# Second block's up projections: one 512-column matmul for both parts of the activation, and a reduction that adds the halves

## The reference, cut to what matters

```python
def swiglu(h, w_gate, w_up, w_down):
    return (jax.nn.silu(h @ w_gate) * (h @ w_up)) @ w_down
...
        h = rmsnorm(x, norm_ffn_pre[layer])
        f = swiglu(h, ffn_w_gate[layer], ffn_w_up[layer], ffn_w_down[layer])
        x = x + rmsnorm(f, norm_ffn_post[layer]).astype(x.dtype)
```

## Time and profile before

| | |
|---|---|
| time, median of 3 runs (lowest to highest) | 1777.63 us (1777.48 to 1779.65) |
| the profiled execution: its own time, its span | 1778.24 us, 1776.3 us |
| granted TensorE clock, mean over the span | 0.981 of full |
| TensorE busy (matmul) | 1696.2 us, 95% |
| TensorE weight loads (beside the matmuls) | 1645.0 us, 93% |
| VectorE busy | 1167.0 us, 66% |
| ScalarE busy | 812.7 us, 46% |
| GpSimd busy | 237.9 us, 13% |
| DMA, mean | 157 GB/s |

### The profile page before, as it was taken

The page is one execution under the profiler, slowest core; times in us unless marked ns, Lnnn a source line. Parts: engine busy times, 40 slices in busy tenths (PEclk is TensorE's granted clock), DMA queues, the critical chain, the costliest instruction groups (busy, mean ns, idle before and its releaser), DMA issues.

```text
span 1776.3 us, 31965 instructions
## 1 busy us (share of the span) xinstructions
PE 1696.2 (95%) x13256; PEld 1645.0 (93%) x13256; DVE 1167.0 (66%) x1590; ACT 812.7 (46%) x1058; POOL 237.9 (13%) x212
## 2 busy tenths in 40 slices
PE   7999999999999999999999996999999999889998
PEld 6999999899999999998899995988999998889997
DVE  5556597686556755587586645566866578677664
ACT  5333473563335433373563434663434355354343
POOL 1002400310032001400220041221100020020000
PEclk9999999999999999999999998998999999999998
DMA  5455443344544555443355552342455533144551
GB/s 209 165 181 186 166 151 119 119 166 166 196 178 152 175 177 187 167 153 119 120 191 185 196 194 92 126 149 98 144 186 209 191 121 107 64 144 175 186 210 74
DMA packets 37298, 279.57 MB, mean 157 GB/s; under 512 B 4320, under 2 KB 4448, under 8 KB 7120
## 3 DMA queue, kind: packets, MB, share of 16 engines
q1 hardware_dynamic: 35440, 269.63, 42.7%
q0 software_dynamic: 1760, 8.56, 1.4%
HBM read 277.13 MB, written 1.05 MB: 157 GB/s over the span
## 4 chain that ended last, share of the span: by engine, by line
PE 76%; DVE 10%; ACT 8%; issue 3%; DMA 1%; POOL 1%; SPq 0%; ACTq 0%; DVEq 0%; POOLq 0%
PE bank L712 24%; PE bank L714 23%; PE bank L713 23%; ACT w_hi L1458 4%; DVE w_lo L2087 4%; DMA raw<-in_up_w 1%; ACT h L1522 1%; ACT h_hi L1521 1%; PE bank L1071 1%; POOL h L648 1%; PE bank L1096 0%; PE bank L1023 0%; PE bank L1256 0%; PE bank L1321 0%; DVE win L2519 0%
## 5 line engine op out<-in xcount | busy, mean ns | idle before, releaser
L2087 DVE TENSOR_TENSOR w_lo<-raw,w_hi 128x2048 fp32r<-128x2048 f32 (+4 forms) x235 | 576.1, 2452 | 278.3 <-ACT w_hi L1458 278.1
L712 PE MATMUL bank<-h_hi,w_hi 128*128 128x256 f32 (+1 forms) x2304 | 663.8, 288 | 20.7 <-DVE h_lo L2243 10.0
L714 PE MATMUL bank<-h_hi,w_lo 128*128 128x256 f32 (+1 forms) x2304 | 660.1, 287 | 0.0
L713 PE MATMUL bank<-h_lo,w_hi 128*128 128x256 f32 (+1 forms) x2304 | 658.7, 286 | 0.0
L1458 ACT ACTIVATE w_hi<-raw 128x2048 fp32r<-128x2048 f32 (+3 forms) x238 | 477.2, 2005 | 314.2 <-PE bank L714 185.3
L712 PEld LDWEIGHTS bank<-h_hi,w_hi 128*128 128x128 f32 x2304 | 438.1, 190 | 27.3 <-issue 16.3
L714 PEld LDWEIGHTS bank<-h_hi,w_lo 128*128 128x128 f32 x2304 | 438.0, 190 | 0.0
L713 PEld LDWEIGHTS bank<-h_lo,w_hi 128*128 128x128 f32 x2304 | 437.1, 190 | 0.1
L712 PE MATMUL bank<-g_hi,w_hi 128*128 128x256 f32 (+1 forms) x1312 | 377.9, 288 | 15.9 <-DVE y L2295 4.0
L714 PE MATMUL bank<-g_hi,w_lo 128*128 128x256 f32 (+1 forms) x1312 | 373.1, 284 | 0.0
L713 PE MATMUL bank<-g_lo,w_hi 128*128 128x256 f32 (+1 forms) x1312 | 372.9, 284 | 0.0
(11 more groups left out here) (371 smaller groups left out, 1894.6 us busy)
## 6 DMA issues: line engine op xcount, KB each, us to landing
raw<-in_up_w SPq DMA_DIRECT2D x111, 1024.0 KB, 4.8
raw<-in_down_w SPq DMA_DIRECT2D x48, 1408.0 KB, 5.8
raw<-in_in_w SPq DMA_DIRECT2D x20, 1024.0 KB, 4.8
raw<-in_up_w SPq DMA_DIRECT2D x16, 1152.0 KB, 5.1
raw<-in_out_w SPq DMA_DIRECT2D x16, 1024.0 KB, 4.8
raw<-in_even_w SPq DMA_DIRECT2D x12, 1024.0 KB, 4.8
raw<-in_odd_w SPq DMA_DIRECT2D x6, 1024.0 KB, 4.8
diag<-in_conv_w POOLq DMA_DIRECT2D x4, 1024.0 KB, 5.1
```

The lines of the kernel that those rows point to most:

```text
L712: pe.matmul(out, w[0], x[0], start=first, stop=False)
L713: pe.matmul(out, w[0], x[1], start=False, stop=False)
L714: return pe.matmul(out, w[1], x[0], start=False, stop=last)
L2087: last = dve.tensor_tensor(lo[:, b:n], raw[:, slot, b:n], hi[:, b:n].bitcast(F32), ALU.subtract)
```

## The change

`h_hi` and `h_lo` become the two halves of one tensor `h_both`. In the chunks 2 to 21 of `ffn_s` the high weight is multiplied with both in a single matmul: 256 columns of the high part and 256 of the low part, into the 512 columns of the bank. The low weight with the high activation is added to the first 256 columns. A bank then holds two halves whose sum is the projection, and VectorE adds them with a `tensor_reduce` over the two (new function `added`) ahead of the gate's multiplication (into `q2`) and ahead of the product's (into `gf`). A semaphore, `halves_added`, takes the place of one that was not used, so that VectorE's next instruction waits for the sum. Chunks 0 and 1 stay as they were.

```diff
-        h_hi = place("h_hi", [P, KD * T], F32R)
-        h_lo = place("h_lo", [P, KD * T], F32R)
+        h_both = place("h_both", [P, 2, KD * T], F32R)
+        h_hi, h_lo = h_both[:, 0], h_both[:, 1]
...
                     for e in range(2):
                         for k in range(KD):
-                            last = mm3(ps[b + e][:, 0:S], wpair(st.wslot(j), 2 * k + e), hpair(k, 0, S),
-                                       k == 0, k == KD - 1)
+                            hi, lo = wpair(st.wslot(j), 2 * k + e)
+                            pe.matmul(ps[b + e][:, :], hi, h_both[:, :, k * T:k * T + S], start=k == 0, stop=False)
+                            last = pe.matmul(ps[b + e][:, 0:S], lo, hs(h_hi, k, 0, S), start=False, stop=k == KD - 1)
...
+                def added(bank, out, nth):
+
+
+                    dve.tensor_reduce(out, bank[:, :].rearrange("p (a n) -> p n a", a=2), AX.X, ALU.add)\
+                        .then_inc(halves_added, 1)
+                    dve.wait_ge(halves_added, seen.at(halves_added, nth))
+                    return out
+
                 def gate(i, j, c):
                     b = 2 * c if c in (2, 3) else 2 * j
                     dve.wait_ge(chunk_used, st.value(j, i, 2))
-                    dve.tensor_tensor(q2[:, j, :], ps[b][:, 0:S], inv_s[:], ALU.mult).then_inc(q_ready, 1)
+                    both = ps[b][:, 0:S] if c in (0, 1) else added(ps[b], q2[:, j, :], i * 4 + (2 * j - 3))
+                    dve.tensor_tensor(q2[:, j, :], both, inv_s[:], ALU.mult).then_inc(q_ready, 1)
 
                 def product(i, j, c):
                     b = 2 * c if c in (2, 3) else 2 * j
+                    both = ps[b + 1][:, 0:S] if c in (0, 1) else added(ps[b + 1], gf[:, j, 0:S], i * 4 + (2 * j - 2))
                     dve.wait_ge(silu_ready, seen.at(silu_ready, i * 2 + (j + 1)))
-                    dve.tensor_tensor(gf[:, j, 0:S], sig[:, j, 0:S], ps[b + 1][:, 0:S], ALU.mult).then_inc(up_free, 1)
+                    dve.tensor_tensor(gf[:, j, 0:S], sig[:, j, 0:S], both, ALU.mult).then_inc(up_free, 1)
```

More of the change, by code:

```diff
@@ L479, in forward @@
         qd_ready = sem("qd_ready")
-        qd_copied = sem("qd_copied")
+        halves_added = sem("halves_added")
         qd_roped = sem("qd_roped")
@@ L2420, in ffn_s @@
                 pairs_of(dve, FT, up, 6)
+                seen.skip(halves_added, 2 * (FT - 2))
                 for s in (silu_ready, up_free, g_hi_done):
```

## The result

The changed kernel is slower. Its median is 1784.61 us (6 runs) against 1778.2 us for the kernel before (6 runs), ratio 1.0033, 95% interval 1.0020 to 1.0045. The ratios are estimates from all runs and need not equal the quotient of the two medians. The measured 1784.61 lies within the stated range of 1776.5 to 1792, and the direction is the one forecast; it is 2.4 us above the forecast of 1782.2 and just above the 1780.8 to 1784 that the forecast gave to itself.

What follows compares the result with a forecast made beforehand. TensorE, busy 95% of the span, was taken to bound the kernel. Per stage 1.64 - 0.07 + 0.74 = 2.3 us, twice that 4.6, added to the median 1777.63 gives 1782.2; range 1776.5 to 1792.

Steps and rivals of the forecast that it cites:

- merged matmul, a chunk: TensorE, chunks 2 to 21: one 512-column matmul replaces two of 256, a chunk goes from 5.68 to 5.60 us.
- reduction: VectorE adding a bank's halves: 0.69 us; 0.73 with its wait in straight code, 0.82 in the loop.
- chunk 5 later, counted from chunk 2: Stage start: w_lo(5) queues behind added reductions on VectorE, so chunk 5 starts 1.20 us later than before.
- chunk 7 later, counted from chunk 2: Loop entry: chunk 6, waiting for gf(4), starts 1.62 us later, so the stage enters the loop 1.64 late.
- loop, mean of a chunk: Steady loop: chunks alternate between 5.65 and 5.70 us, 5.675 each, a gain of 0.1 per stage.
- first down chunk, wait at block 20: Stage end: TensorE waits for g_lo of chunk 21, 0.64 us plus 0.10 for the wait, 0.74.
- a stage: Each of the second block's two feed-forward stages: 1.64 - 0.07 + 0.74 = 2.3 us slower.
- latency sum of 5.65: Loop: from chunk c-1's first matmul to release of c-2's banks, 5.65 us against TensorE's 5.60, so TensorE waits 0.05.
- Cheap and slow sums: Rivals on the reduction: 0.42 us, giving 1775.8, chance 0.11; or 1.0 us, VectorE bounding, giving 1799, chance 0.10.
- calm loop: Rival: loop release comes in time or its wait costs no refill, chunks take 5.60, total 1780.2; chance 0.20.
- The clock: Rival: TensorE's idle before chunk 5, grown to 2.0 us, lowers its granted clock, total 1785.4; chance 0.10.
- fast wide matmul: Rival: 512-column matmuls run well under 0.232 us, VectorE sets the turn at 5.43, total 1774.9; chance 0.03.

Runs made afterwards that it cites:

- e2: Kernel before with merged matmuls in chunks 2 to 21 but no sums, one product left out: 1776.24 us against 1778.34, ratio 0.9988.
- e7: Change in chunks 6 to 19 only, product's reduction moved ahead of w_lo, against the kernel before: 1777.64 us against 1778.83, ratio 1.0001.
- e4: Change in chunks 6 to 19 only, other chunks as in the kernel before: 1778.47 us against 1778.34, ratio 1.0000.
- e5: Change in chunks 6 to 21 only, chunks 2 to 5 as in the kernel before: 1778.36 us against 1778.83, ratio 0.9999.
- e6: Change in chunks 2 to 19 only, chunks 20 and 21 as in the kernel before: 1784.15 us against 1778.83, ratio 1.0029.
- e9: The second measurement: the full changed kernel again, beside the kernel before: 1782.94 us against 1779.04, ratio 1.0020.
- e8: Change in chunks 4 to 20, product's reduction moved ahead of w_lo, against the kernel before: 1776.28 us against 1778.83, ratio 0.9986.
- e3: Three 256-column matmuls per block as before, second into the bank's other half, VectorE adds the halves: 1785.57 us against 1778.34, ratio 1.0042.
- e1: Kernel before with only h_hi and h_lo made halves of one tensor: 1777.86 us against 1778.34, ratio 0.9998.
- e10: Repeat of e8, chunks 4 to 20 with the reduction ahead of w_lo: 1776.68 us against 1779.04 for the kernel before, ratio 0.9985.

## Why the prediction was right

The mechanism and its sum held: each place was where the text had it, and the stages cost 4.4 us against 4.6. The median moved by 6.4, and the 2 us beyond the stages are in no step of the forecast; the second measurement, 3.9 between the medians, lies below the sum, so the two leave no clear rest.

| step | forecast | measured |
|---|---|---|
| merged matmul, a chunk | 5.60 us | 5.59 (e2) |
| reduction | 0.69, with its wait 0.73, in the loop 0.82 | 0.68 to 0.69, 0.73, 0.81 |
| chunk 5 later, counted from chunk 2 | 1.20 | 1.05 and 1.29 |
| chunk 7 later, counted from chunk 2 | 1.64 | 1.66 and 1.67 |
| loop, mean of a chunk | 5.675 | 5.67 (chunks 7 to 21 in 79.32 and 79.41) |
| first down chunk, wait at block 20 | 0.74 | 0.70 |
| a stage | 2.3 | 2.13 and 2.25 |
| sum | 4.6 | 4.4 |

- *The matmul and the reduction* were taken from rows of the same form and came out as these rows. The figures of the Trainium skill (TensorE: Matmul & The Clock Gate, Back-to-back issue gap) did not hold for these matmuls: the wide one is followed after 0.23 us, not after 0.131 nor 0.216.
- *The loop* does what the latency sum of 5.65 said: TensorE waits in every second chunk. The changed kernel's timeline at one of these starts shows both parts of the cost, the wait (the chunk's first matmul follows after 0.18 us in place of 0.12) and the refill (the second one after 0.34 in place of 0.23):

```profile
1301.91 0.28 PE L829 MATMUL bank<-h_both,w_lo 128*128 128x256 f32 x1
1302.09 0.51 PE L828 MATMUL bank<-h_both,w_hi 128*128 128x512 f32 x1
1302.43 0.28 PE L829 MATMUL bank<-h_both,w_lo 128*128 128x256 f32 x1
```

  That it is the latency, shown by e7 against e4, was the part of the argument that a sum of busy times would have missed: 5.43 us of VectorE's work in a chunk of 5.60. The same sum says how little room is left: between chunks 7 and 21 of the first stage w_lo waits for w_hi 21.3 us in all before and 1.9 in the changed kernel.
- *The start and the end* were each followed instruction by instruction, and e5 and e6 put them where the text had them, 1.7 and 0.6 a stage. Chunk 5 differs between the stages (1.05 and 1.29) because chunk 2 does: it took 6.22 us in the first stage of before and 6.03 in that of the changed kernel, 6.11 and 6.14 in the second. In the first stage chunk 7 had one more hold-up: w_hi of chunk 7 waited for its weights, because the later w_lo(5) had freed their slot late and because this load took 6.6 us; in e9 it was issued equally late, took 5.8 and held nothing up. The forecast did not have it; it cost 0.2 us there and nothing in the second stage. So the 1.66 of the first stage is in part luck: chunk 5 was 0.15 less late than forecast, and the hold-up made up for it (1.47 in e9's first stage, which has none).
- *The rivals.* Cheap and slow sums fell with the 0.69. The calm loop fell, the waits are there. The clock did not fall in the profiled wait of 1.95 us before chunk 5, nor in that of 2.0 in the second stage. The stretch around the first shows it (PEclk is the number after the last bracket):

```profile
1276.00:1294.00 18.00, 15.71 (x87) 13.04 (x86) 16.72 (x23) 7.17 (x7) 0.00 (x0) 1.00 0.52 177
```

  The row that the prediction holds against this, 0.56 over 1440 to 1446, is not from the wait that it names: it stands behind a wait of 3.29 us ahead of the second layer's mixer. The wait ahead of the second layer's feed-forward stage is 2.89 us, up to 1571.42, and the granted clock over 1570 to 1574 was 0.50. So the clock fell at the longer waits and not at those of 1.95 and 2.0. The fast wide matmul fell with e2, at 5.59 us a chunk.

## What to carry to other kernels

Here, work added to an engine with time to spare was free only where its idle time lay. Before adding it, write down the loop from the release of a buffer to its reuse, and put the work on the side of the wait that is already there: the same two reductions cost the gain of the loop behind w_lo (e4) and nothing ahead of it (e7). A gain per turn has to pay for the turns in which the pipeline fills and drains, where the engine that idles in the loop can be the late one, as VectorE was; leaving those turns as they were (e4 to e8) costs a few conditions in the code.

## What the runs showed of the hardware that was not expected

- A release that comes 0.1 us ahead of the matmul that waits for it still costs 0.07 us at the next matmul, one that comes 0.16 us ahead costs nothing (e3). The loop before the change has its release 0.9 us ahead.
- The load of up weights ahead of the first stage took 4.98 us in the profile of before, 6.04 in e1 and 6.20 in the changed kernel, for the same load. Together with the granted clock in stretches ahead of it (0.90 over 1100 to 1120 and 0.67 over 1210 to 1220 before, 0.74 and 0.52 in e10) this moved the start of chunk 2 between 1257.1 and 1262.2 us over the profiles, while a stage with the same code repeats within 0.13 us where no load is late. A change of 0.2% is better read from such a cut than from a few medians, as long as the time of the whole program is shown beside it.
- Most long loads have a transfer of instructions in them. Of the 572 loads of 1 MB of up weights after 1200 us in the thirteen profiles, 502 had no 16 KB transfer of an instruction queue in their first 4.7 us: they took 4.74 us in the median, and two of them more than 5.2. Of the 70 that had one, 32 took more than 5.2, the longest 7.0. That the transfer is the cause was not tested by a run of its own.
